# Seven-product stage of a transformer kernel: other places for five steps around its first pair of tiles

## The reference, cut to what matters

```python
hn = rms_norm_2(h, ffn_norm[l])
h = h + (jax.nn.silu(hn @ w_gate[l]) * (hn @ w_up[l])) @ w_down[l]
```

## Time and profile before

| | before |
|---|---|
| median of 3 runs | 1878.49 us (1875.58 to 1878.83) |
| profiled execution, its own time | 1875.84 us |
| its span | 1874.0 us |
| TensorE busy in the span | 1791.4 us (96%) |
| VectorE, ScalarE, GpSimd busy | 58%, 42%, 18% |
| mean granted TensorE clock | 0.976 |

### The profile page before, as it was taken

One profiled execution on the slowest core, in us unless ns is written; L12 is line 12 of the kernel. 1 busy time (PEld: TensorE's weight loads), 2 busy tenths in 40 slices (PEclk: granted clock), 3 DMA queues, 4 the chain that ended last, 5 costly groups with the idle time before them and its releaser, 6 DMA issues.

```text
span 1874.0 us, 23947 instructions
## 1 busy us (share of the span) xinstructions
PE 1791.4 (96%) x9595; PEld 1470.2 (78%) x9595; DVE 1090.4 (58%) x1690; ACT 781.3 (42%) x1329; POOL 338.5 (18%) x285
## 2 busy tenths in 40 slices
PE   7999999999999999989999999899979999999998
PEld 5778877788888877778888888797756688999887
DVE  6778855444454365455777742565356568888322
ACT  4433344432334453343443432435357535555221
POOL 2014501011212140041111110230010022332100
PEclk9999999999999999999999999999979899999999
DMA  5222322132224431112322222131211144775521
GB/s 192 79 90 90 102 91 79 68 113 90 93 97 144 143 111 54 46 56 90 113 90 90 99 101 93 68 136 46 98 68 33 46 157 113 186 192 141 186 90 57
DMA packets 58464, 188.82 MB, mean 101 GB/s; under 512 B 6955, under 2 KB 9643, under 8 KB 58225
## 3 DMA queue, kind: packets, MB, share of 16 engines
q1 hardware_dynamic: 47664, 160.15, 25.4%
q0 software_dynamic: 10112, 26.62, 5.6%
q10 hardware_dynamic: 576, 0.52, 0.1%
HBM read 180.97 MB, written 6.29 MB: 100 GB/s over the span
## 4 chain that ended last, share of the span: by engine, by line
PE 81%; DVE 7%; ACT 5%; issue 4%; POOL 2%; DMA 1%; SPq 0%; DVEq 0%; POOLq 0%; ACTq 0%
PE ps L400 25%; PE ps L402 24%; PE ps L401 24%; PE ps L405 3%; PE ps L3007 2%; ACT ws_h L328 1%; DVE ws_l L336 1%; POOL sums L448 1%; PE ps L3024 1%; POOL x L1468 1%; DMA s<-in_ffn_up 1%; DMA x<-in_x 0%; ACT P L3133 0%; DVE tmp L842 0%; PE ps L3019 0%
## 5 line engine op out<-in xcount | busy, mean ns | idle before, releaser
L336 DVE TENSOR_TENSOR ws_l<-raw,ws_h 128x1024 fp32r<-128x1024 f32 x255 | 354.3, 1395 | 402.2 <-ACT ws_h L328 401.8
L400 PE MATMUL ps<-h_h,ws_h 128*128 128x512 f32 (+1 forms) x1176 | 474.4, 403 | 19.8 <-DVE h_l L575 9.8
L401 PE MATMUL ps<-h_l,ws_h 128*128 128x512 f32 (+1 forms) x1176 | 462.6, 393 | 0.0
L402 PE MATMUL ps<-h_h,ws_l 128*128 128x512 f32 (+1 forms) x1176 | 462.4, 393 | 0.0
L328 ACT ACTIVATE ws_h<-raw 128x1024 fp32r<-128x1024 f32 x255 | 267.4, 1053 | 323.1 <-PE ps L402 318.8
L400 PEld LDWEIGHTS ps<-h_h,ws_h 128*128 128x128 f32 x1176 | 225.2, 191 | 82.0 <-issue 15.9
L402 PEld LDWEIGHTS ps<-h_h,ws_l 128*128 128x128 f32 x1176 | 225.2, 192 | 49.6
L401 PEld LDWEIGHTS ps<-h_l,ws_h 128*128 128x128 f32 x1176 | 226.2, 192 | 45.3
L400 PE MATMUL ps<-fb_h,ws_h 128*128 128x256 f32 x476 | 134.5, 282 | 3.6 <-DVE ws_l L2302 2.6
L402 PE MATMUL ps<-fb_h,ws_l 128*128 128x256 f32 x476 | 134.4, 282 | 0.0
L401 PE MATMUL ps<-fb_l,ws_h 128*128 128x256 f32 x476 | 133.9, 281 | 0.0
(11 more groups left out here) (486 smaller groups left out, 3119.0 us busy)
## 6 DMA issues: line engine op xcount, KB each, us to landing
raw<-in_ffn_up SPq DMA_DIRECT2D x88, 512.0 KB, 3.5
raw<-in_w_merge SPq DMA_DIRECT2D x36, 512.0 KB, 3.4
raw<-in_ffn_down SPq DMA_DIRECT2D x22, 512.0 KB, 3.5
raw<-in_w_down SPq DMA_DIRECT2D x22, 512.0 KB, 3.6
raw<-in_w_hy SPq DMA_DIRECT2D x12, 512.0 KB, 4.1
raw<-in_w_sc SPq DMA_DIRECT2D x12, 512.0 KB, 3.5
s<-in_ffn_up SPq DMA_DIRECT2D x17, 256.0 KB, 4.1
s<-in_ffn_up POOLq DMA_DIRECT2D x17, 256.0 KB, 5.1
```

The lines of the kernel that those rows point to most:

```text
L336: dve.e.tensor_tensor(w.lo, raw[n % NRAW][:], w.hi, ALU.subtract).then_inc(*lo_made.says(("lo", n)))
L400: pe.e.matmul(o, a.hi, b.hi, start=start, stop=False, skip_group_check=True)
L401: pe.e.matmul(o, a.hi, b.lo, start=False, stop=False, skip_group_check=True)
L402: return pe.e.matmul(o, a.lo, b.hi, start=False, stop=stop, skip_group_check=True)
```

## The change

Both orders around pair 5 change. On ScalarE, `made_hi2(2)` and `s1_hi(5)` go ahead of `silu(3)`. On VectorE, `evacuate(3)` moves behind S1 lo(5), S2's sum and `made_lo2(2)`. The gate tile of unit 4 is evacuated behind `s4_add(5)`, ahead of `s3_lo(5)`. Its up tile is evacuated right behind w(5), and `made_lo2(3)` follows it. `behind_splits` is gone. GpSimd, SyncE and TensorE keep their orders. The diff is whole:

```diff
--- before.py
+++ after.py
@@ -2131,10 +2131,10 @@
         a1_hi(CLASSIC)
         operand_first(5, ("xs", 3), *(("parked again", m) for m in range(4)))
         operand_first(6, ("T4", "made"), ("xs", 7), *(("parked again", m) for m in range(4, 8)))
+        made_hi2(2)
+        s1_hi(CLASSIC)
         silu(3)
-        s1_hi(CLASSIC)
         s2_hi(CLASSIC)
-        made_hi2(2)
 
         def among_first():
             silu(CLASSIC - 1)
@@ -2268,19 +2268,15 @@
         a1_lo(CLASSIC)
         operand_rest(5)
         operand_rest(6)
-        evacuate(3)
         s1_lo(CLASSIC)
         s2_add(CLASSIC)
+        made_lo2(2)
+        evacuate(3)
         s2_lo(CLASSIC)
         s4_add(CLASSIC)
+        evacuate(4, (0,))
         s3_lo(CLASSIC)
-        made_lo2(2)
-
-        def last_of_classic():
-            evacuate(CLASSIC - 1, (1,))
-            made_lo2(CLASSIC - 2)
-
-        fast_dve(lambda: evacuate(CLASSIC - 1, (0,)), last_of_classic)
+        fast_dve(lambda: evacuate(4, (1,)))
         f = Follow(chunk_dve)
         for m in range(8):
             f.next(22)
@@ -2336,7 +2332,7 @@
         w = ws_a2()[:, 512:1024]
         dve.e.tensor_tensor(w.lo, raw_a2(p)[:, 512:1024], w.hi, ALU.subtract).then_inc(*half_lo.says(("A22 lo", p)))
 
-    def fast_dve(behind_w, behind_splits):
+    def fast_dve(behind_w):
 
         def c22(p):
             dve.wait_ge(("done", ("M7", p)), ("w", p), ("gone", ("n8", p - 2, 1)))
@@ -2358,8 +2354,7 @@
             dve.e.tensor_tensor(w_at, m1_of(p), out_of(("R", p))[:, 0:256], ALU.subtract).then_inc(*dve_out.says(("w", p)))
             if p == CLASSIC:
                 behind_w()
-            else:
-                made_lo2(p - 2)
+            made_lo2(p - 2)
             dve.wait_ge(("done", ("M6", p)), ("m1", p), ("c12", p - 1) if p > CLASSIC else None)
             dve.e.tensor_tensor(y_at, out_of(("Q", p))[:, 0:256], m1_of(p), ALU.subtract).then_inc(*dve_out.says(("y", p)))
             s4_lo(p)
@@ -2367,9 +2362,7 @@
                 s1_lo(p + 1)
                 s2_add(p + 1)
                 a1_lo(p + 1)
-            if p == CLASSIC:
-                behind_splits()
-            else:
+            if p > CLASSIC:
                 c21(p - 1)
             if p == LAST:
                 down_lo(1)
```

## The result

| | before | changed |
|---|---|---|
| median of 6 runs each | 1877.72 us (1875.58 to 1878.83) | 1868.94 us (1866.09 to 1872.81) |
| ratio | | 0.996, interval 0.9945 to 0.9976 |
| profiled execution, its own time | 1875.84 us | 1868.28 us |
| span | 1874.0 us | 1866.5 us |
| mean granted clock | 0.976 | 0.979 |

The change makes the kernel faster by 0.4%, with an interval of 0.24% to 0.55%. The two profiled spans differ by 7.5 us, of which 2.2 lie ahead of the change: M1(5) starts at 1564.09 instead of 1566.29. From there to the end of the span it is 307.7 us before and 302.4 changed, **5.3 us less**.

The account below looks back on a forecast made before the run. TensorE, busy 96% of the span, was taken as the bound, stalling before M6(6) and M1(7). M1(7) starting 3.3 us earlier plus 1.6 us from full clock made 4.9 us: 1878.49 to 1873.6 us, range 1870.0 to 1877.7.

Parts of the forecast that it names:

- the forecast's own range: Whole kernel: 1872.3 (no idle at M1(7), no rest at M6(6)) to 1875.0 us (late S4 lo(5), 0.9 at M2(7)).
- the most: TensorE's losses at M6(6) (1.15 us), M1(7) (2.79) and 17 slow-clock matmuls (1.6): 5.5 us in all.
- the 1.6 us: TensorE behind the long stall before M1(7): 17 matmuls at 0.212 instead of 0.118 us would run at full clock.
- The evacuation and the two gates: Unit 4's up tile done at 1570.6 instead of 1575.08; adding DMA, next held by silu(4) and glu(4), only 2.1 us earlier.
- S4 lo(5): VectorE step ahead of M3(5): ends about 1572.2, making TensorE wait a new 0.4 us (bounds 0 and 0.7).
- The adding DMA's time: GpSimd's DMA for pair 7, ahead of M1(7): 6.2 us taken, between median 5.1 and worst 7.4.
- The lock between VectorE and GpSimd: Shared ports: a VectorE step started within glu ends 0.56 us after it; without such a lock, gain 0.5 larger.
- The slow DMA: Rival, chance 0.20: pair 7's adding DMA still takes 7.4 us, M1(7) starts at 1586.6; gain 3.7 us, 1874.8.
- the wait at M2(7): Rival, chance 0.17: late S3(7) DMA stalls M2(7) 0.9 us and the clock falls again; gain 2.4 us, 1876.1.
- the slower side: Rival, chance 0.05: busy VectorE delays the adding DMA's descriptors to 11 us, M1(7) 1.5 us later than before; 1880.0.

Follow-up runs that it names:

- The second comparison: The changed kernel, unaltered, measured again against the kernel before on a second chip: 1871.67 against 1874.82 us, ratio 0.9981, stretch 302.3 us.
- ScalarE's edit alone: Kernel before with only ScalarE's order changed (made_hi2(2) and S1 hi(5) ahead of silu(3)), VectorE's order untouched: ratio to before 1.001, stretch 308.6 us.
- up tile back: Changed kernel with one step undone, unit 4's up tile evacuated behind A1 lo(6) again: ratio to before 0.9999, stretch 308.1 us.
- other buffer: Kernel before, all orders kept, with pair 7's row buffer in other memory so SyncE's load waits for earlier matmuls: ratio to before 0.9968, stretch 303.4 us.
- late part: Kernel before with only VectorE's late moves (unit 4's tiles and made_lo2(3) about their new places): ratio to before 0.9996, stretch 303.0 us.
- up tile later: Changed kernel with unit 4's up tile and made_lo2(3) behind S4 lo(5) instead of w(5): ratio to before 0.9992, stretch 304.0 us.
- silu(4) early: Changed kernel with silu(4) ahead of S1 hi(6) and A1 hi(6) on ScalarE: ratio to before 0.9982, stretch 303.5 us.
- more room: Changed kernel with pair 7's adding DMA issued ahead of glu(4) and made_lo2(3) behind S4 lo(5): ratio to before 0.9975, stretch 302.4 us.

## Why the prediction was right

The forecast was 1873.6 us, a gain of 4.9 (0.26%). The median came out at 1868.94, which is 1.1 us below the range of 1870.0 to 1877.7. The ratio of 0.996, taken from the 1878.49 that the forecast starts from, gives 1871.0, which lies within it. In the part that the change touches, the gain is 5.3 us by the profiles, and there the forecast's mechanism held. The rest of the 8.8 us between the medians was not forecast. The second comparison, with 3.2, has less than the stretch, so how much of the 5.3 a median shows is not settled by these runs.

Two sizes of the range were off. It allowed 3 us for how far runs of one kernel differ, by three runs, and 35 runs spread over 12. The low end of the forecast's own range, 1872.3, is 6.2 us below 1878.49, more than the 5.5 that the prediction calls the most.

**What can be gained.** 5.5 us were forecast as the most. The changed stretch without its 0.16 us is 302.25, and before lies 5.46 above it. The terms close in other kernels too: with 0.094 us for each slow matmul, ScalarE's edit alone comes to 1.13 + 3.61 + 1.5 = 6.2 over 302.25, and 6.3 was measured; the up tile back comes to 4.38 + 1.2 = 5.6 and measured 5.8.

**The clock.** With waits of 0.78, 1.13 and 1.79 us it stayed at 1.00; behind 2.79, 3.61 and 4.38 it fell (behind the 3.61 the first nine matmuls still ran at 1.00). That the 1.6 us came with the long wait and went with it is shown by the other buffer, where that wait alone was removed and 4.3 us were gained for 2.8 us of wait. Between 1.79 and 2.79 us no run had a wait.

**The evacuation and the two gates.** Forecast +4.3 for its end, measured +4.2; the adding DMA at +9.6, measured +9.3. That glu(4) and silu(4) come next behind SyncE's gate is shown by the other buffer, where the load was ready 8.6 us earlier and only 1.2 us of it reached the DMA.

**S4 lo(5).** Forecast 0.4 us lost, measured 0.16: VectorE came to w(5) at +3.2 instead of +3.3, and the steps behind it took a little less than my rounded ones. This term was too large by 0.24.

**The adding DMA's time.** 6.2 us were taken and 5.8 measured; M1(7) has 0.2 us to spare instead of 0.3 to wait. This term was too large by 0.3. With the 0.24 of S4 lo(5) that makes 0.5, and the gain is 0.4 above the forecast's 4.9. The time of this DMA fell into three groups in the ten profiles, and they go with the moment at which SyncE issues its load of A2 of pair 7:

| kernels | A2 load issued, us behind the adding DMA | adding DMA takes |
|---|---|---|
| before, up tile back, ScalarE only | -0.6, -2.0, -1.1 | 7.4, 7.3, 7.7 |
| changed (twice), other buffer, late part | 0.6, 0.7, 0.6, 0.6 | 5.8, 5.6, 5.8, 6.0 |
| up tile later, silu(4) early, more room | 1.2, 2.6, 2.9 | 4.5, 4.3, 4.2 |

That fits the prediction's reason, that SyncE's transfers move out from under it. No run varied it alone: the adding DMA of pair 8 moves too, and is issued 0.9 to 1.6 us behind this one in the second group and 2.3 to 2.5 in the third.

**The lock between VectorE and GpSimd.** It held in each case: A22 lo(5), started at 1572.36 within glu(4), took 1.62 and ended 0.55 behind it. The price of 0.5 us that I put on it against a kernel without a lock was not measured by itself.

**The rivals.** The slow DMA, the wait at M2(7) and the slower side did not come: the 0.37 us at S3 hi(7) stayed on ScalarE. Nor did the clock fall once more.

**What the sum did not hold.** The medians of the first comparison differ by 8.8 us. In the profile pair 2.2 of 7.5 us lie ahead of M1(5). The windows there show TensorE's clock a little higher in the changed kernel's execution, 0.98 against 0.97 up to 1560 us:

```profile
0.00:1560.00 1560.00, 1487.79 (x7523) 1189.78 (x7524) 904.47 (x1395) 651.07 (x1120) 269.73 (x221) 0.97 0.28 93
```

```profile
0.00:1560.00 1560.00, 1489.12 (x7532) 1189.60 (x7533) 906.96 (x1397) 652.63 (x1122) 269.70 (x221) 0.98 0.29 93
```

In ten profiles M1(5) starts between 1564.1 and 1571.2 us, and the changed kernel alone has both 1564.1 and 1569.0. So the surplus over 5.3 us is most likely chance of that part. The clock goes with it over all runs: in the 35 runs of before on either chip, the time falls as the mean granted clock rises, with a correlation of -0.87 and -0.80 and by 1.0 to 1.1 us for each 0.001. Why the clock is lower in one execution than in another stays open.

## What to carry to other kernels

When buffers share memory with something that others still read, look for the last reader and for who is queued behind the DMA that waits for it: here one 0.68 us evacuation, placed 4.6 us too late, cost 5.6 us of TensorE when it alone was put back. Behind the gate that the chain of waits names stands the next one, so cost a moved step by the next gate and not by how far it moved. And where the end of a second stall is set by something that the first doesn't hold, removing the first only lengthens the second.

## What the runs showed of the hardware

- A VectorE step with two operands in SBUF that starts within a GpSimd tensor_tensor step of 128 x 512 (1.3 us alone) ended 0.54 to 0.56 us behind it at 512 columns and 1.07 to 1.10 at 1024, in every case that the ten profiles show one by one between 1540 and 1860 us (36 and 53). Steps of 128 x 256 with one operand in PSUM took 0.41 to 0.42 us within such a step, as they do outside. A 1024-column step that started 0.01 us ahead had GpSimd wait instead (2.36 us for a 1.3 us step).
- The same adding DMA of 256 KB took from 4.2 to 7.7 us in the ten profiles, and less where SyncE's next 512 KB load was issued later (the table above).
- One kernel's executions differ by up to 12 us (before: 1870.66 to 1882.69 over 35 runs on one chip). A fixed stretch of the profile differed by 0.1 us between the two profiles of the changed kernel, and 0.5 us came in by the clock of its last matmuls in one other kernel.
